# A two-layer float32 block on one core: the boundary behind the experts done tile by tile, with the output gate's product first

## The reference

```
y = segment_sum(y_rows * row_w)              # two expert rows for each token, weighted
x = x + y                                    # "x2" in the kernel
x = rmsnorm(x, norm_final_g)                 # end of the first block: "x3"
u = rms_norm(x, a_norm_g) @ a_w_in           # the mLSTM layer's input product
xm, om, gates, zm, xp, zp = split(u)
xc = silu(causal_conv(xm, conv_w, conv_b))
q, k = xc @ w_q, xc @ w_k;  v = xm @ w_v
i_pre, log_f = gates[..., :4], log_sigmoid(gates[..., 4:])   # scans over the 512 tokens
hm = mlstm(q, k, v, i_pre, log_f) * sigmoid(om)
x = x + concat([ya, yb]) @ w_out
```

## Time and profile before

| | us |
|---|---|
| median of the runs | 1812.13 |
| runs | 1816.89, 1812.13, 1811.68 |
| the profiled execution | 1809.11 |
| its span in the trace | 1807.3 |
| TensorE busy in the span | 1666.9 (92%) |
| VectorE busy | 747.5 (41%) |
| ScalarE busy | 615.5 (34%) |
| GpSimd busy | 135.5 (7%) |

### The profile page before, as it was taken

One profiled execution on the slowest core, in us unless ns is written; L12 is line 12 of the kernel. 1 busy time (PEld: TensorE's weight loads), 2 busy tenths in 40 slices (PEclk: granted clock), 3 DMA queues, 4 the chain that ended last, 5 costly groups with the idle time before them and its releaser, 6 DMA issues. The chain is left out here.

```text
span 1807.3 us, 21308 instructions
## 1 busy us (share of the span) xinstructions
PE 1666.9 (92%) x8347; PEld 1219.6 (67%) x8347; DVE 747.5 (41%) x1395; ACT 615.5 (34%) x1072; POOL 135.5 (7%) x200
## 2 busy tenths in 40 slices
PE   6999999999999798887878787899999999999899
PEld 5888888888888653332323233688788888988777
DVE  3544345544564611010101001772546743446782
ACT  4123225444441401111110111654444232457760
POOL 0000001001000001111111110010002000000330
PEclk9999999999999899999998999899999999999999
DMA  7665364653236679999999997332123232322101
GB/s 149 88 102 95 104 94 71 69 66 62 63 111 252 258 287 422 420 421 421 421 422 422 422 421 306 132 105 94 47 70 94 94 141 86 95 72 76 69 2 70
DMA packets 127413, 325.93 MB, mean 180 GB/s; under 512 B 8213, under 2 KB 81685, under 8 KB 118608
## 3 DMA queue, kind: packets, MB, share of 16 engines
q1 hardware_dynamic: 121520, 313.76, 53.0%
q0 software_dynamic: 4784, 8.13, 1.2%
q10 hardware_dynamic: 1008, 2.65, 0.4%
HBM read 317.97 MB, written 14.69 MB: 184 GB/s over the span
## 5 line engine op out<-in xcount | busy, mean ns | idle before, releaser
L1991 DVE TENSOR_TENSOR w_lo<-w_raw,w_hi 128x2048 fp32r<-128x2048 f32 (+1 forms) x72 | 156.9, 2180 | 285.1 <-ACT w_hi L909 277.4
L909 ACT ACTIVATE w_hi<-w_raw 128x512 fp32r<-128x512 f32 (+3 forms) x138 | 169.8, 1252 | 291.2 <-DMA w_raw<-in_w_in 106.0
L1729 PE MATMUL bank<-gate,xt 128*64 128x512 f32 x512 | 231.0, 605 | 28.2 <-DMA up<-in_w_e_up 28.2
L1730 PE MATMUL bank<-up,xt 128*64 128x512 f32 x512 | 231.5, 606 | 0.0
L2313 DVE TENSOR_TENSOR gated_h<-gu_silu,bank 64x512 f32<-64x512 f32 x32 | 22.1, 690 | 403.4 <-ACT gu_silu L1121 403.4
L1729 PEld LDWEIGHTS bank<-gate,xt 128*64 128x64 f32 x512 | 70.0, 140 | 172.3 <-issue 172.3
L1752 PE MATMUL bank<-down,hT 128*64 128x512 f32 x256 | 131.8, 664 | 25.7 <-DVE hT L2320 25.7
L1419 PE MATMUL bank<-h1T_hi,w_hi 128*128 128x512 f32 x376 | 151.0, 401 | 0.0
L1421 PE MATMUL bank<-h1T_hi,w_lo 128*128 128x512 f32 x376 | 147.2, 391 | 0.0
L1420 PE MATMUL bank<-h1T_lo,w_hi 128*128 128x512 f32 x376 | 146.8, 390 | 0.0
L1753 PE MATMUL bank<-down,hT 128*64 128x512 f32 x256 | 131.8, 664 | 0.0
(11 more groups left out here) (686 smaller groups left out, 3635.9 us busy)
## 6 DMA issues: line engine op xcount, KB each, us to landing
down<-in_w_e_down SPq DMA_DIRECT2D x32, 2048.0 KB, 35.0
up<-in_w_e_up SPq DMA_DIRECT2D x30, 2048.0 KB, 31.7
gate<-in_w_e_gate SPq DMA_DIRECT2D x30, 2048.0 KB, 32.7
w_raw<-in_w_in SPq DMA_DIRECT2D x24, 1024.0 KB, 9.8
w_raw<-in_a_w_in SPq DMA_DIRECT2D x20, 1024.0 KB, 5.4
w_raw<-in_w_in SPq DMA_DIRECT2D x16, 512.0 KB, 10.3
w_raw<-in_a_w_out SPq DMA_DIRECT2D x8, 1024.0 KB, 5.0
w_raw<-in_w_conv_out SPq DMA_DIRECT2D x4, 1024.0 KB, 5.4
```

The source lines that it names most:

```text
L909: return nc.scalar.activation(out, in_, ACT.Copy, scale=scale)
L1729: g_ins = pe.matmul(out[0:CAP, :], x, ring_gate[p][:, c, :], start=c == 0, stop=c == KC - 1)
L1730: u_ins = pe.matmul(out[CAP:, :], x, ring_up[p][:, c, :], start=c == 0, stop=c == KC - 1)
L1991: V.tensor_tensor(ring_view(w_lo, n), ring_view(raw, n), ring_view(w_hi, n).bitcast(F32), ALU.subtract)\
```

## The change

- **Order of the dense products.** Before: `xm`, `gates`, `om`, `v2`. Now: `om`, `xm`, `gates`, `v2`. The slices of weights are listed, loaded and split in the new order.
- **By tiles.** The boundary is no longer done for four tiles at once. For each tile: sum, gain, two sums of squares, variances, root, Newton step, `x2n_tok` as one operation of VectorE with the gain `a_norm_g` in it (`ga`, a row of 1024 broadcast to 128 partitions, loaded beside `gfin`), 8 transposes (`turn_x2`) into two banks, high and low parts. The first half of `om` is multiplied between the transposes, tile by tile (`om_part`).
- **Who sums.** Tile 0: VectorE. Tiles 1 and 2: TensorE (`TILES_ON_PE`), in PSUM pairs of their own. Tile 3: GpSimd, five operations of 128x1024 right behind `moe_done`, one after the other.
- **Loads.** The expert rows come in the order 0, 1, 2, 3, into two other buffers; a second small gain copy to DRAM (`gain2_dram`) is made with the first, and `ga` is loaded from it.
- **x3** is written over `x2g_tok` and stored from there, behind the last tile's transposes and before the `om` sigmoids on ScalarE.
- **Splits.** ScalarE splits the first slice before it takes the last expert's rows, the second behind them, the third behind `moe_done`; VectorE the first two before `moe_done`, the third behind the last tile.
- **Gate chain.** VectorE starts it right behind the last convolution; ScalarE's Exp and Ln come in the middle of the `v2` results and the second Exp behind them.

```
-TILES2, TILE_ON_PE = (0, 2, 1, 3), 1
+TILES_ON_PE = (1, 2)
+OM_BANKS, TURN_BANKS = ((1, 5, 2, 4), (0, 3, 6, 7)), ((0, 3), (6, 7))
...
             nc.gpsimd.memset(pool_mark[:, 1:2], 0).then_inc(moe_done, 1)
+            last = TT - 1
+            for k, y_tok in enumerate((y1_tok, y2_tok)):
+                pool.wait_ge(sem(f"y{k + 1}_loaded{last}"), 16)
+                step(nc.gpsimd.tensor_tensor(y_tok[:, last, :], y_tok[:, last, :], tok_w[:, k, last:last + 1].to_broadcast([P, D]), ALU.mult))
+                ins = nc.gpsimd.tensor_tensor(x1_tok[:, last, :], x1_tok[:, last, :], y_tok[:, last, :], ALU.add)
+                if k == 0:
+                    step(ins)
+            ins.then_inc(sem("last_x2_made"), 1)
+            pool.wait_ge(sem("last_x2_made"), 1)
+            nc.gpsimd.tensor_tensor(x2g_tok[:, last, :], x1_tok[:, last, :], gfin[:, :], ALU.mult).then_inc(sem("last_x2_made"), 1)
...
+            x2_squares(0)
+            x2g_squares(0)
+            take_root(2, 0)
+            for tt in range(1, TT):
+                x2_squares(tt)
+                x2T_high(tt - 1)
+                x2g_squares(tt)
+                take_root(2, 2 * tt)
+            x2T_high(TT - 1)
...
+            def x2_factors(tt):
+                a, b = 2 * tt, 2 * tt + 1
+                dve.wait_ge(ssq_made, before2 + b + 1)
+                step(V.tensor_scalar(var[:, a:a + 1], ssq[:, a:a + 1], 1.0 / D, EPS, ALU.mult, ALU.add))
+                step(V.tensor_scalar(ssum[:, a:a + 1], ssq[:, b:b + 1], 1.0 / D, None, ALU.mult))
+                norms[0] += 1
+                V.scalar_tensor_tensor(out=var[:, b:b + 1], in0=var[:, a:a + 1], scalar=EPS, in1=ssum[:, a:a + 1],
+                                       op0=ALU.mult, op1=ALU.add).then_inc(var_made, 1)
+                newton_steps(2, a)
+                V.scalar_tensor_tensor(out=x2n_tok[:, tt, :], in0=x2g_tok[:, tt, :], scalar=rstd[:, b:b + 1], in1=ga[:, :],
+                                       op0=ALU.mult, op1=ALU.mult).then_inc(sem("x2n_made"), 1)
...
+            for tt in range(TT):
+                ins = om_part(tt, 0)
+                if tt + 1 < TT:
+                    turn_x2(tt + 1)
+                else:
+                    ins.then_inc(sem("half_used"), 1)
+                om_part(tt, 1).then_inc(results, 1)
+            token_wide("om", 1, 512, [(hT_hi[1], hT_lo[1], 0), (hT_hi[1], hT_lo[1], 4)])
```

More of the change, by code:

```diff
@@ L501, in build_kernel @@
         a_in = t["a_w_in"]
+        for n in range(2):
+            add_wide("om", n, cols_of(a_in, D + 512 * n, 512), KC, 512)
         for s in range(4):
@@ L1160, in _, with x2_squares @@
[L1160 to L1164, removed]
-            for tt in range(TT):
-                copy(x1_tok[:, tt, :], x2g_tok[:, tt, :], r_fin[:, tt:tt + 1]).then_inc(sem("x3_made"), 1)
+            split(slices1 + 2, n_slices)
+            def x2_squares(tt):
+                if tt in TILES_ON_PE:
+                    act.wait_ge(sem("x2_summed"), TILES_ON_PE.index(tt) + 1)
+                    squares(x2_psum[tt][:, :], junk2[:, :], 2 * tt)
+                else:
+                    act.wait_ge(sem("x2_made" if tt == 0 else "last_x2_made"), 1)
+                    squares(x1_tok[:, tt, :], junk2[:, :], 2 * tt)
@@ new lines, in x2g_squares, with x2T_high @@
+            def x2g_squares(tt):
+                if tt == TT - 1:
+                    act.wait_ge(sem("last_x2_made"), 2)
+                else:
+                    act.wait_ge(sem("x2g_made"), tt + 1)
+                squares(x2g_tok[:, tt, :], junk2[:, :], 2 * tt + 1)
+            def x2T_high(tt):
+                for h in range(2):
+                    src = until_made(act, ("x2T", h, tt))
+                    copy(hT_hi[1][:, 4 * h:4 * h + 4, tt * P:(tt + 1) * P], src[:, :].rearrange("p (c n) -> p c n", c=4)).then_inc(hi_made, 1)
@@ L1167, in conv_silu @@
+            for tt in range(TT):
+                om_out(0, tt)
+            act.wait_ge(sem("half_used"), half_turn[("om", 0, 0)])
+            split(slice_no[("om", 1, 1)], n_slices)
+            split(slice_no[("xm", 0)], n_slices)
+            act.wait_ge(sem("half_used"), half_turn[("om", 1, 0)])
+            split(slice_no[("xm", 1)], n_slices)
+            for tt in range(TT):
+                om_out(1, tt)
             def conv_silu(j):
@@ L1181, in _ @@
             split(slice_no[("gates", 0)] + 2, n_slices)
[L1182 to L1200, removed]
+            act.wait_ge(x3_stored, 16 * TT)
             copy(v2[:, :, :, MD:], const[:, C_ONE:C_ONE + 2 * TT * MH].rearrange("p (t h n) -> p t h n", t=TT, h=MH))
@@ L1779, in _ @@
             pe.wait_ge(moe_done, 1)
[L1781 to L1787, removed]
@@ L2088, in _, with log_gate @@
                 split(slice_no[("gconv", s)] + 2, slices1)
-            def log_gate(src, low, x, ab, logs, one, bias, made, log_made):
+            def log_gate(src, low, x, ab, logs, one, bias, made, log_made, meanwhile=None):
                 step(V.tensor_copy(x[:, :], low))
@@ L2389, in _ @@
                 h_copy(e)
+            split(slices1, n_slices)
+            split(slices1 + 1, n_slices)
             count, _ = over_values(dve)
@@ new lines, in x2T_low @@
+            def x2T_low(tt):
+                at_ = slice(tt * P, (tt + 1) * P)
+                for h in range(2):
+                    src = until_made(dve, ("x2T", h, tt))
+                    his[0] += 1
+                    dve.wait_ge(hi_made, his[0])
+                    took(V.tensor_tensor(hT_lo[1][:, 4 * h:4 * h + 4, at_], src[:, :].rearrange("p (c n) -> p c n", c=4),
+                                         hT_hi[1][:, 4 * h:4 * h + 4, at_].bitcast(F32), ALU.subtract), ("x2T", h, tt))
@@ new lines, in _ @@
+            x2_add(0)
+            x2_gained(0)
+            x2_factors(0)
+            x2_gained(1)
+            x2T_low(0)
+            x2_factors(1)
+            x2_gained(2)
+            x2T_low(1)
+            x2_factors(2)
+            x2T_low(2)
+            x2_factors(3)
+            x2T_low(3)
+            split(slices1 + 2, n_slices)
+            dve.wait_ge(sem("half_used"), half_turn[("om", 0, 0)])
+            split(slice_no[("om", 1, 1)], n_slices)
+            split(slice_no[("xm", 0)], n_slices)
```

196 lines of the change are left out of this document (108 added, 88 removed).

## The result

| | us |
|---|---|
| changed kernel, median (lowest to highest) | 1826.96 (1825.44 to 1828.21) |
| kernel before, in the same comparison | 1813.85 (1811.68 to 1816.89) |
| ratio, 95% interval | 1.0072 (1.0057 to 1.0087) |
| predicted | 1812.1 (1802.5 to 1817.5) |
| the profiled execution of the changed kernel; its span | 1828.21; 1826.4 |

The changed kernel is 0.72% slower, 13.1 us (10.3 to 15.8). The forecast was no change, with 0.13 for slower, and the measured time lies above its range.

What follows compares the result with a forecast made beforehand. TensorE, busy in 92% of the span, was taken as the bound, so only its waits could give time. Terms -0.7 + 1.4 - 1.3 + 0.6 = 0.0, carried to the median: 1812.1 us, range 1802.5 to 1817.5.

Steps and rivals of the forecast that it cites:

- The gate chain itself costs nothing: Behind the last xm: the chain takes some 20 us while v2, q2 and k2 occupy TensorE over 30; 0.0.
- The second gain copy lies in SP's wait for the next slice's turn: In SP's queue of loads: the extra copy to DRAM falls into an existing wait and costs nothing.
- The hold: Tile 1's norm: VectorE operations with two SBUF inputs wait for GpSimd's operation to end, turning -9.4 into -0.7.
- the one tie: Tile 1's Newton step against GpSimd's next start: x2n ready at 1148.4 or 1151.2, middle 1149.8 taken; -2.1 to +0.7.
- The clock behind the wait: Behind TensorE's wait for tile 1's x2n: the next 4.5 us run at half clock, 2.2 us lost.
- The pipeline's own -9.4: Boundary of experts and dense products: by tiles, without the hold, dense work begins in effect 9.4 us earlier.
- The rival without the hold: Tile 1's norm: VectorE is not held on operations of one or two columns; sum -8.7, 1803.4; chance 16%.
- the one with slower GpSimd operations: Tile 3 on GpSimd: each of five operations takes 3.4 us, tile 1's x2n comes later; +5.7, 1817.8; chance 14%.
- Behind the gates: End of xm: the last convolution ends after the gate matmuls, without om to cover it; +1.4.
- The table load: First head's exponentials: the table for Exp is already in place, so its 1.28 us load leaves the path; -1.3.
- `ga`: Ahead of the experts' stream: another 0.5 MB to load, about half of which may fit; +0.6 (0 to 1.25).
- om's late slice: om's second half: its weight slice fits with about 2.5 us to spare; 0, or 2 if its load is late.

Runs made afterwards that it cites:

- experiment 1: Changed kernel with PSUM bank 0 given back right behind VectorE's last read of the gates, not behind neg_m: 1816.35 us, ratio 1.0014.
- experiment 2: Changed kernel with tile 3's two adds and its product with gfin on VectorE, GpSimd idle there: 1818.25 us, ratio 1.0029.
- kernel 4: Changed kernel with both bank 0 given back early and tile 3 summed and scaled on VectorE: 1809.39 us, ratio 0.9984.
- experiment 6: Kernel before, plus the second gain copy at 180 us, read by nothing, and the g_ffn load waiting for both copies: 1814.59 us, ratio 1.0021.
- 8: kernel 4 with v2 waiting for xm's low parts alone, and the second gain copy moved from 180 to 530 us: 1803.84 us, ratio 0.9954.

## Why the prediction was wrong, point by point

**The step that failed** is "The gate chain itself costs nothing: some 20 us behind the last xm, while v2, q2 and k2 occupy TensorE for over 30." I asked when the chain's results are needed, and these are indeed needed late. I did not ask what the chain holds until then. It holds bank 0, which the eighth v2 result asks for 12 us behind the gates (1252.3 to 1264.3). The term at 0.0 was an estimated +9.4 from the trace (7.1 of wait, 2.3 of half clock) and 8.9 to 10.6 in experiments 1, 2 and 4.

**A second term was missed**: "The second gain copy lies in SP's wait for the next slice's turn [...]: nothing." It does lie there and does not delay the next issue. Its price is 3.8 us (1.8 to 5.6) in experiment 6, where the medians have only 2.2, and 3.7 to 4.0 in 8; it shows at transfers 150 us later. With 9.4 and 3.8 put in, 0.0 becomes 13.2; measured is 13.1 (10.3 to 15.8). That the two agree to 0.1 is luck: each of the two terms is known to 1 or 2 us, and smaller ones were off too.

**The hold was there, and its end came out right in part by luck.** x2n of tile 1 was to be ready 24.0 to 26.8 us behind the end of the experts (1148.4 to 1151.2 less 1124.4); it was at 24.7 (1159.56 less 1134.91). But the way there was another. The joined variance, forecast to wait for GpSimd's second operation, ran into the third (1151.35 against its start at 1151.29), and from there each wait came one GpSimd operation later than forecast. VectorE won the one tie, of 0.03 us (1155.66 against 1155.69), and still x2n came behind the fifth operation, the slower of the two forecast outcomes, 26.8. That it was ready at 24.7 is because GpSimd was faster: it took 1.89 to 2.38 for each and was through 11.6 us after its start (1146.45 to 1158.03), where the forecast had 13.2 (1136.7 to 1149.9, or 2.6 for each and not the 2.5 that it names). Two errors cancelled.

The one-input Newton operation was held by the fifth (1155.85). The Trainium skill's rule (GPSIMD Engine Reference, Key points), under which operations in a 2-port mode wait too, agrees with this row, 2.20 us in place of 0.17; the trace of before had shown nothing of it. Here it changed little, since the next operation has two SBUF inputs. The clock behind the wait cost 2.0, forecast 2.2.

**What the hold and the pipeline were worth.** The forecast put the hold at 8.7 us (-9.4 against -0.7). From the mark to the end it is 7.1, and 7.0 in experiments 1 and 4; only the medians of experiment 2 give 8.7. The pipeline's own -9.4 was too large by about as much: in kernel 4, with both losses gone and tile 3 on VectorE, the part behind the mark is 7.4 us shorter than before (682.9 less 675.5), where the terms without the hold sum to -9.3. So in experiment 1, with the hold in place, the forecast of -0.6 (-0.7, +1.4, -1.3) against a measured 0 within the spread is again two errors that cancel. The rival without the hold (16%) is not what happened, nor is the one with slower GpSimd operations (14%), though that one ended as slower.

**The small terms.** Behind the gates: forecast +1.4, measured 1.8. The table load: forecast -1.3; the first Exp of the heads now starts 0.78 us behind mdiag's start and was 2.05 behind it, so it comes 1.27 earlier; no run tests what that is worth in time. These rows answer to the earlier trace rows:

```profile
1302.14 0.69 DVE L2598 TENSOR_TENSOR mdiag<-x_psum,const 128x512 f32<-128x512 f32 x1
1302.92 0.40 ACT L1271 ACTIVATE wexp<-mdiag,cols 128x128 f32<-128x128 f32 x1 [3.46 <-DVE mdiag L2598]
```

`ga`: forecast +0.6, not to be told from 0 in three comparisons. om's late slice: no wait of TensorE from 1180 to 1210, as forecast.

**What stays open**: why a copy of 4 KB in small pieces at 180 us makes transfers at 335 to 350 longer. From 335 to 350 the DMA share is 0.90 to 1.04 at 35 to 80 GB/s in the traces with the copy and without, so they are slow ones anyway. No run here separates what the copy changes for them, and none has a copy of 4 KB in one piece, so it isn't shown either that the small pieces do it and not simply one more transfer ahead on the queue. Also why six of the eight traces with the copy, and none of the five without it, spend 1.6 us more between 465 and 535 us.

## What to carry to other kernels

When a step is moved closer to its consumer, list what it holds and until when, buffers and banks as well as results, and look who asks for each next in the new order: a bank signalled free at the end of a chain was harmless with 43 us of work in between and cost 9 with 12. Signal a buffer free behind its last read. A second engine's help is to be priced with what its operations keep the first one from doing: five GpSimd operations stood over 11 us beside a chain of tiny VectorE operations and cost 7 to 9 us, where VectorE itself did the work in under 4 without TensorE noticing. And take a second trace of the kernel before ahead of reading a few microseconds off two traces, and compare the stretch that the change touches and not only the whole.

## What the runs showed of the hardware that I had not expected

- One-input operations are held or not. TENSOR_SCALAR on 128x1 ran for 0.15 us in the middle of a GpSimd operation (1150.98, GpSimd from 1148.84 to 1151.22), on 128x2 it was held for 2.20 until GpSimd's end (1155.85). It was so in three traces. The two differ in width, but the second also writes over its input, and no run varies one of these alone. RECIPROCAL on 128x2 was not held (0.17, at 1153.54 beside GpSimd's 1153.26 to 1155.61), nor was a product of 128x1024 with one input in PSUM (1.23, at 1147.82 beside GpSimd's 1146.45 to 1148.76).
- A large operation is held as well. In experiment 1 VectorE's x2n, 128x1024, met the fifth GpSimd operation and took 3.25 us in place of 1.28:

```profile
1149.61 2.35 POOL L895 TENSOR_TENSOR x2g_tok<-x_tok,gfin 128x1024 f32<-128x1024 f32 x1
...
1149.79 3.25 DVE L2519 SCALAR_TENSOR_TENSOR x2n_tok<-x2g_tok,rstd,ga 128x1024 f32<-128x1024 f32 x1
```

- A DMA of 4 KB issued at 180 us cost 2.2 to 4.0 us of time (experiments 6 and 8), and what it delays shows 150 us behind it. With it issued at 530 us the experts' mark stands at 1125.8 and 1126.5, among those of the order before (1124.4 to 1126.6, without the copy).
